# Differential attention on one core: v and z of a head pair projected together in row layout, rows gated before they are transposed, the weighting of values moved into the next pair

## The reference

```
proj = u @ w_in                                  # 2048 x 8192: q | k | v | z
logits = q_h @ k_h.T * scale + bias, causal      # 16 heads of 128 columns
p = softmax(logits)                              # two heads make a pair
a = p[:, :, 0] - lam * p[:, :, 1]
o = rms_norm(a @ v, subln_g) * (1 - lam_init)    # v: 256 columns for each pair
y = (o * silu(z)) @ w_out
h = layer_norm(alpha * x + y, ln_g, ln_b)
```

## Time and profile before

| | |
|---|---|
| median of 3 runs | 979.56 us (979.45 to 979.62) |
| profiled execution | 979.38 us |
| its span, first to last instruction | 977.6 us |
| TensorE busy | 963.7 us, 99% |
| VectorE busy | 449.1 us, 46% |
| ScalarE busy | 310.5 us, 32% |
| GpSimd busy | 66.4 us, 7% |
| granted TensorE clock, mean | 0.996 |

### The profile page before, as it was taken

How to read it: one execution, slowest core, us unless ns; L and a number is a source line. 1 busy time by engine, 2 the same in 40 slices (tenths; PEclk the granted TensorE clock), 3 DMA queues, 4 the chain that set the end, 5 groups by cost and what they waited for, 6 DMA issues and landing times.

```text
span 977.6 us, 13295 instructions
## 1 busy us (share of the span) xinstructions
PE 963.7 (99%) x5200; PEld 836.1 (86%) x5200; DVE 449.1 (46%) x694; ACT 310.5 (32%) x493; POOL 66.4 (7%) x137
## 2 busy tenths in 40 slices
PE   9999999999999999999999999999999999999995
PEld 7898889888988898889888988898889888888884
DVE  4634443454345434543454345334533475425465
ACT  4424322432243224322432243223322453122200
POOL 2000100010001000100010001000100010000044
PEclk9999999999999999999999999999999999999998
DMA  8722422242224222322242224222322224442432
GB/s 293 269 89 84 135 87 88 85 134 86 86 86 134 86 86 86 134 86 86 86 135 86 86 86 134 86 86 86 107 86 86 86 76 139 174 149 87 150 115 101
DMA packets 32790, 108.63 MB, mean 111 GB/s; under 512 B 4208, under 2 KB 5232, under 8 KB 32512
## 3 DMA queue, kind: packets, MB, share of 16 engines
q1 hardware_dynamic: 28320, 94.65, 28.3%
q0 software_dynamic: 2336, 9.48, 2.9%
q10 hardware_dynamic: 2112, 4.19, 1.3%
HBM read 104.07 MB, written 9.48 MB: 116 GB/s over the span
## 4 chain that ended last, share of the span: by engine, by line
PE 98%; ACT 0%; POOL 0%; DMA 0%; DVE 0%; issue 0%; POOLq 0%; ACTq 0%
PE proj L774 81%; PE att L774 15%; PE att L858 1%; PE att L883 1%; DMA big<-x_cols_dram 0%; POOL big L384 0%; POOLq L73 0%; POOL var_eps L376 0%; ACT x_res L418 0%; ACT w_split L525 0%; ACT scratch L416 0%; ACT big L539 0%; DVE stats L726 0%; DVE big L723 0%; DVE xg_split L555 0%
## 5 line engine op out<-in xcount | busy, mean ns | idle before, releaser
L774 PE MATMUL proj<-xg_split,w_split 128*128 128x512 f32 x2304 | 539.9, 392 | 0.4 <-DVE w_split L668 0.3
L774 PEld LDWEIGHTS proj<-xg_split,w_split 128*128 128x128 f32 x2304 | 428.4, 188 | 87.8 <-DVE xg_split L555 0.6
L549 DVE TENSOR_TENSOR w_split<-w_raw,w_split 128x1024 fp32r<-128x1024 f32 x128 | 156.8, 1225 | 279.9 <-ACT w_split L397 279.0
L397 ACT ACTIVATE w_split<-w_raw 128x1024 fp32r<-128x1024 f32 x128 | 135.6, 1059 | 442.6 <-PE proj L774 434.0
L774 PE MATMUL proj<-w_split,xg_split 128*128 128x256 f32 (+1 forms) x1872 | 265.3, 302 | 0.0
L774 PEld LDWEIGHTS proj<-w_split,xg_split 128*128 128x128 f32 x1872 | 249.4, 191 | 13.5
L591 DVE CUSTOM_DVE_ANT_0 scratch<-att,bias 128x128 f32<-128x128 f32 (+3 forms) x64 | 28.9, 489 | 108.4 <-PE att L774 108.4
L774 PE MATMUL att<-operands 128*128 128x256 f32 (+2 forms) x432 | 71.2, 303 | 0.0
L774 PE MATMUL att<-w_split,xg_split 128*128 128x512 f32 x288 | 66.1, 389 | 0.0
L774 PEld LDWEIGHTS att<-operands 128*128 128x128 f32 x432 | 61.5, 190 | 3.1
L774 PEld LDWEIGHTS att<-w_split,xg_split 128*128 128x128 f32 x288 | 54.1, 188 | 11.2
(11 more groups left out here) (73 smaller groups left out, 409.1 us busy)
## 6 DMA issues: line engine op xcount, KB each, us to landing
w_raw<-w_in_tiles_dram SPq DMA_DIRECT2D x126, 512.0 KB, 3.3
w_raw<-w_out_tiles_dram SPq DMA_DIRECT2D x32, 512.0 KB, 3.3
bias_by_distance<-bias_lines POOLq DMA_DIRECT2D x8, 640.0 KB, 6.4
bias<-bias_by_distance POOLq DMA_DIRECT2D x8, 512.0 KB, 5.4
x_res<-in_x_dram ACTq DMA_DIRECT2D x4, 1024.0 KB, 5.1
big<-x_cols_dram SPq DMA_DIRECT2D x7, 512.0 KB, 9.8
out_dram<-big SPq DMA_DIRECT2D x4, 512.0 KB, 2.7
out_dram<-big SPq DMA_DIRECT2D x8, 256.0 KB, 2.5
```

Of the source, the lines that this page charges most:

```text
L397: nc.scalar.activation(split_view(a, 0), w_raw[:, ring(a)], ACT.Copy).then_inc(w_hi, 1)
L549: nc.vector.tensor_tensor(split_view(a, 1), w_raw[:, ring(a)], split_view(a, 0).bitcast(F32), ALU.subtract).then_inc(w_ready, 1)
L774: return nc.tensor.matmul(dst, lhsT, rhs, start=start, stop=stop, skip_group_check=True)
```

## The change

1. v and z of a pair are made together. Their weight tiles are stored anew: 8 tiles of two blocks of 128 rows, each 512 columns wide, 256 of v and 256 of z. `vz_part` (quarters j = 8 to 15) keeps rows of x stationary and moves 512 columns, 24 matmuls a quarter, for one block of rows s after another; block s has the whole bank s of `proj`. So z is now in row layout too.
2. The gate is applied to rows: `gate` on DVE reads the weighted values from PSUM, the row norm's scale and silu(z), and writes `gated`; ACT's second pass over the weighted values is gone. Then `turn_gated` transposes two blocks at once, and ACT copies them to `g` with the gain `subln_g` (`g_copy`).
3. `weigh_v` of a pair moves to quarters 0 to 3 of the next pair, `turn_a` for t = 2, 3 to its quarters 0 and 1, `turn_gated` to 3 and 5. `turn_a` for t = 0, 1 stands after quarter 12.
4. ACT copies z, exp(-z) and v of a block as soon as the block is finished (`vz_tiles`), DVE the lo part of v. k is moved head by head.
5. `scores_of(0)` makes 128 columns.
6. In the layer norm `var_eps` goes from POOL to DVE, the gain is copied by ACT into the `proj` banks and for the last block the bias into `att`, and the DVE's pieces are 512 + 1024 columns (centre) and 3 x 512 (scale).
7. The last pair's slots are written out after the loop on DVE and ACT, with the first splits of g in slot 14.

The core of the diff:

```diff
-                    if c == 2:
-                        for s in range(ST):
-                            rows = slice(s * P, (s + 1) * P)
-                            dst = proj[:, bank + s // 2, (s % 2) * PW:(s % 2 + 1) * PW]
-                            mm(dst, x_hi[:, rows], w[0][:, kk], first and s % 2 == 0, False)
-                            mm(dst, x_hi[:, rows], w[1][:, kk], False, False)
-                            last = mm(dst, x_lo[:, rows], w[0][:, kk], False, final and s % 2 == 1)
+            def vz_part(p, j):
+                part = j - VZ
+                pe.wait_ge(w_ready, p * QUARTERS + j + 1)
+                w = [split_view(j, l).rearrange("p (k n) -> p k n", k=VK) for l in range(2)]
+                for s in range(ST):
+                    if part == 0:
+                        if s == 0:
+                            pe.wait_ge(q_moved, p + 1)
+                        elif s >= 2:
+                            pe.wait_ge(k_moved, 2 * p + s - 1)
+                    rows = slice(s * P, (s + 1) * P)
+                    dst = proj[:, s]
+                    for kk in range(VK):
+                        k = part * VK + kk
+                        x_hi, x_lo = xg_split[:, 0, k, rows], xg_split[:, 1, k, rows]
+                        mm(dst, x_hi, w[0][:, kk], k == 0, False)
+                        mm(dst, x_hi, w[1][:, kk], False, False)
+                        last = mm(dst, x_lo, w[0][:, kk], False, k == KT - 1)
...
+                if part == 0 and not opening:
+                    pe.wait_ge(vz_moved, p * ST - 2 + 2 * c)
...
-                n = max(t + 1, 2) * P
+                n = (t + 1) * P
...
             def late_inserts(p, j):
-                if j == 0:
-                    weigh_v(p, 3)
-                if j < 4:
-                    turn_normed(p, j)
+                if j < ST:
+                    weigh_v(p, j)
+                if j < 2:
+                    turn_a(p, j + 2)
+                if j in (3, 5):
+                    turn_gated(p, j // 2 - 1)
 
             def own_inserts(p, j):
                 if 9 <= j < 13:
                     scores_of(p, j - 9)
-                if 11 <= j < 15:
-                    turn_a(p, j - 11)
-                if 13 <= j:
-                    weigh_v(p, j - 13)
+                if j == 12:
+                    turn_a(p, 0)
+                    turn_a(p, 1)
...
+            def vz_tiles(p):
+                for s in range(ST):
+                    if s < ST - 1:
+                        act.wait_ge(vz_done, p * (ST - 1) + s + 1)
+                    else:
+                        act.wait_ge(quarter_done, (p + 1) * QUARTERS)
+                    nc.scalar.activation(silu_z[:, s], proj[:, s, PW:2 * PW], ACT.Exp, scale=-1.0)
+                    nc.scalar.activation(z_rows[:, s], proj[:, s, PW:2 * PW], ACT.Copy)
+                    nc.scalar.activation(v[:, 0, s], proj[:, s, 0:PW], ACT.Copy).then_inc(vz_hi, 1)
...
+                dve.wait_ge(o_scale_ready, n)
+                dve.wait_ge(silu_ready, n)
+                nc.vector.scalar_tensor_tensor(gated[:, t], av, o_scale[:, t:t + 1], silu_z[:, t],
+                                               ALU.mult, ALU.mult).then_inc(gated_ready, 1)
...
-                pool.wait_ge(mv_ready, s + 1)
-                nc.gpsimd.tensor_scalar(var_eps[:, s:s + 1], mean_var[:, s, 1:2], 1.0, EPS,
-                                        ALU.mult, ALU.add).then_inc(var_ready, 1)
...
+                nc.vector.tensor_scalar(var_eps[:, s:s + 1], mean_var[:, s, 1:2], EPS, None, ALU.add
+                                        ).then_inc(var_ready, 1)
...
                     nc.vector.scalar_tensor_tensor(r_rows[:, s, cols], r_rows[:, s, cols], mean_var[:, s, 0:1],
-                                                   ln_g_all[:, cols], ALU.subtract, ALU.mult).then_inc(centred, 1)
+                                                   bank_cols(g_banks, cols), ALU.subtract, ALU.mult
+                                                   ).then_inc(centred, 1)
```

More of the change, by code:

```diff
@@ L216, in chunk_part, with turned_a @@
         def chunk_part(p, j):
-            if isinstance(p, int) and p == 0 and j < 8:
+            if isinstance(p, int) and p == 0:
                 return j % 2, j // 2
-            return j // 4, j % 4
+            return j // QK, j % QK
+        def turned_a(t):
+            return turned[:, P:3 * P] if t == 1 else turned[:, 0:(t + 1) * P]
         def x_unit_of(k):
@@ L430, in aT_split @@
                     act.wait_ge(av_done, p * ST + t - 1)
-                act.wait_ge(aT_done, p * ST + t + 1)
-                nc.scalar.activation(aT[:, t % 2, 0, 0:(t + 1) * P], turned[:, 0:(t + 1) * P],
-                                     ACT.Copy).then_inc(aT_hi, 1)
+                act.wait_ge(aT_done, p * ST + max(t, 1) + 1)
+                nc.scalar.activation(aT[:, t % 2, 0, 0:(t + 1) * P], turned_a(t), ACT.Copy).then_inc(aT_hi, 1)
             def norm(p, t):
-                if t == 0 and not (isinstance(p, int) and p == 0):
-                    act.wait_ge(g_ready, p * ST)
@@ L446, in late_steps, with g_copy @@
-            def late_steps(p, j):
-                if j == 0:
[L449 to L453, removed]
+            def g_copy(p, i):
+                act.wait_ge(nT_done, 2 * p + i + 1)
+                for e in range(2):
+                    src = turned.rearrange("p (t e s) -> p e t s", t=2, e=2)[:, e]
+                    dst = g[:, bass.ds(p * 2 + e, 1), 2 * i * P:2 * (i + 1) * P]
+                    last = nc.scalar.activation(dst.rearrange("p k (t s) -> p (k t) s", t=2), src, ACT.Copy,
+                                                scale=sub_g[:, e:e + 1])
+                last.then_inc(g_ready, 1)
@@ L454, in own_steps, with slot @@
+            def late_steps(p, j):
+                if j in (1, 2):
+                    aT_split(p, j + 1)
+                if 1 <= j <= 4:
+                    norm(p, j - 1)
+                if j in (4, 6):
+                    g_copy(p, j // 2 - 2)
+            def slot(p, j, late):
+                if j == VZ:
+                    k_chunk(p)
+                split_hi_at(p, j)
+                if late:
+                    late_steps(p - 1, j)
                 if j == (7 if isinstance(p, int) and p == 0 else 4):
-                    chunk(p, 0)
@@ L456, in own_steps, with g_early_hi @@
-                if j in (8, 12):
-                    chunk(p, j // 4 - 1)
+                    q_chunk(p)
+                if j == 13:
+                    aT_split(p, 0)
+                    aT_split(p, 1)
                 if 10 <= j < 14:
                     exps(p, j - 10)
[L460 to L463, removed]
+            def g_early_hi():
+                act.wait_ge(g_ready, (PAIRS - 1) * 2)
+                act.wait_ge(scores_done, PAIRS * ST)
+                for i in range(EARLY // 2):
+                    nc.scalar.activation(g_early[:, 0, 2 * i:2 * i + 2], g[:, 2 * i:2 * i + 2],
+                                         ACT.Copy).then_inc(g_hi, 1)
@@ L535, in _ @@
                         load_res(act, c)
-            for s in range(ST):
+            act.wait_ge(ln_loaded, 32)
+            act.wait_ge(r_ready, (CHUNKS - 1) * ST)
+            for c in range(CHUNKS):
+                last = nc.scalar.activation(g_banks[:, c], ln_g_all[:, c * NC:(c + 1) * NC], ACT.Copy)
+            last.then_inc(ln_moved, 1)
+            for s in range(ST):
+                if s == ST - 1:
+                    act.wait_ge(r_ready, CHUNKS * ST - 1)
+                    for c in range(CHUNKS - 1):
+                        last = nc.scalar.activation(b_banks[:, c], ln_b_all[:, c * NC:(c + 1) * NC], ACT.Copy)
+                    last.then_inc(ln_moved, 1)
                 act.wait_ge(shift_ready, s + 1)
@@ new lines, in k_chunk, with vz_tiles @@
+            def k_chunk(p):
+                for e in range(2):
+                    dve.wait_ge(k_hi, 2 * p + e + 1)
+                    nc.vector.tensor_tensor(kT[:, 1, e], proj[:, 2 + e], kT[:, 0, e].bitcast(F32),
+                                            ALU.subtract).then_inc(k_moved, 1)
+            def vz_tiles(p):
+                for s in range(ST):
+                    dve.wait_ge(vz_hi, p * ST + s + 1)
+                    nc.vector.tensor_tensor(v[:, 1, s], proj[:, s, 0:PW], v[:, 0, s].bitcast(F32),
+                                            ALU.subtract).then_inc(vz_moved, 1)
@@ L600, in combine @@
                 n = p * ST + t + 1
-                if not (isinstance(p, int) and p == 0):
-                    dve.wait_ge(normed_ready, n - ST)
                 dve.wait_ge(exp_ready, n * 2)
@@ L964 @@
 G_ORDER = [*G_STEPS.values(), *G_REST]
-VECTOR_PIECES = [slice(0, D // 2), slice(D // 2, 3 * D // 4)]
+CENTRE_PIECES = [slice(0, NC), slice(NC, 3 * NC)]
+VECTOR_PIECES = [slice(c * NC, (c + 1) * NC) for c in range(CHUNKS - 1)]
 POOL_PIECE = slice(3 * D // 4, D)
```

269 lines of the change are left out of this document (139 added, 130 removed).

## The result

The changed kernel takes 968.52 us (median of 4, 968.31 to 968.76) against 979.55 for the kernel before (979.45 to 979.62): a ratio of 0.9888, interval 0.987 to 0.9905, 11.0 us less. 967.5 was predicted. The profiled execution took 968.76 us, its span is 966.8.

What follows compares the result with a forecast made beforehand. TensorE was taken to bound the eight pairs, and a chain over DVE, POOL, ACT and DMA the end. Terms -10.0 - 0.5 + 0 + 0.8 - 2.3 = -12.0 us gave 967.5 us, range 964.7 to 974.6 (forecast's own 964.7 to 969.5).

Steps and rivals of the forecast that it cites:

- Part 1: v and z quarters of each pair: 96 matmuls fewer save 1.25 us a pair, 10.0 us in all (9.4 to 11.3).
- Part 2: Scores of t = 0: 48 matmuls go from 256 to 128 columns at the transposes' 110 ns, -0.5 us.
- both other prices: For a 128-column matmul: 66 ns by a straight line through 256 and 512 columns, or plain float32's 236 (472 a matmul).
- Part 3: Steps moved within the loop: their results come before TensorE wants them, thinnest cover 0.6 us at the first gate; 0 us.
- T + 2.5: T is the start of the next pair's quarter 0; ACT's last block and the weight split end 2.5 us later.
- Part 4: Last pair's seam with the output product: a 1.4 us wait for the gate replaces one of 0.6; +0.8 us (0.0 to 1.6).
- Part 5: Kernel's end, layer norm: power starts earlier and POOL's two steps take 1.12 us each; -2.3 us (-1.1 to -2.6).
- cheap end: The forecast with the cheap ends of parts 1, 2 and 5: 964.8 us.
- the narrow form: Rivals on the 128-column scores: 236 ns a matmul gives 973.6 us, chance 0.35; 472 ns gives 984.9, chance 0.04.
- the loop's gate: Rival: DVE's queue to the first gate is late in every pair, +13 us, 980.8 at most; chance 0.05.
- columns alone: Rival: columns alone set the matmul time, so the joined v and z quarters gain about 0, 977.5 us; chance 0.03.

Runs made afterwards that it cites:

- cut matmuls: The changed kernel with each joined matmul of 512 columns cut into two of 256, same order of work: 987.29 us.
- in bulk: The changed kernel with quarter 10 of every pair cut into pieces of 128 columns, 96 matmuls instead of 24: 1010.22 us in one run.

## Why the prediction was right

**Part 1, v and z together.** Predicted 1.25 us a pair, 10.0 in all. A pair came out 1.27 to 1.28 us shorter (8.92 / 7), the joined quarters at 5.45. The cut matmuls show the step itself: 12.2 ns a matmul, where 12 to 13 were read from the earlier trace rows. The Trainium skill's 2.5 ns ("TensorE: Matmul & The Clock Gate", section "Back-to-back issue gap") is given there for isolated matmuls and does not hold for this stream; 1536 matmuls at that price would have cost 3.8 us, and they cost 18.8.

**Part 2, the narrow scores.** Predicted -0.5 by the transposes' 110 ns; in bulk it is 112. The choice of the nearest row was right, and both other prices are excluded; but nearness was the only reason given, so that the two agree so well is in part luck. What the term lacked is that the next group gives nearly all of it back (5.54 for 5.47): the gain is nil within what the runs can tell.

**Part 3, the cover.** The queue to the first gate was worked out to end 0.6 us ahead of its need, more with overlap. The timeline of DVE in the changed kernel, the first split of the queue and the gate:

```profile
197.76 1.23 DVE L591 TENSOR_TENSOR w_split<-w_raw,w_split 128x1024 fp32r<-128x1024 f32 x1 [0.52 <-ACT w_split L414]
...
205.59 0.48 DVE L670 SCALAR_TENSOR_TENSOR scratch<-att,o_scale,scratch 128x256 f32<-128x256 f32 x1
```

The gate ends at 205.59 + 0.48 = 206.07, 1.19 us ahead of the six matmuls that want it, which start at 207.26 (1.36 ahead of the end of the quarter before, 207.43). The steps of silu, split and scale took what their rows said. Quarter 0 starts at 195.65, so the queue began 0.4 us sooner than the T + 2.5 of the working, and its steps overlap by 0.2. The banks for quarters 0 and 8 were never waited for. The added reciprocal shows that there was little room here, 1.1 us; that every other place has more was not tried.

**Part 4, the seam.** Predicted a wait of 1.4 us for one of 0.6, +0.8; measured 1.07 of idle and 0.24 of lost overlap, 1.25 by the pair of runs with and without it, for 0.6: +0.7. The cause is the one named, since it goes when the gates stand ahead of the splits. (Of the two splits of g in that queue, the first, from 778.16, runs just ahead of the first row of the order listing of the changed kernel; that listing shows only the second.)

**Part 5, the end.** This term was mis-sized: -2.3 predicted, -1.7 measured, -1.6 by the end alone. POOL was set free as worked out, but its steps take 1.27 us and not 1.12, twice 0.15; and the last transfer takes 966.8 - 963.33 - 0.45 = 3.0 us behind its issue where it was 2.6. The run with the end alone shows 3.0 too, so this comes with the new end; why it lands later was not tried. The working's 2.65 is 0.03 above its own terms (1.22 + 0.93 + 0.47). The Trainium skill's rule on the shared port ("SBUF — State Buffer", section "SBUF: two separate sides") agrees with the runs: with one operand in PSUM DVE takes 2.06 us beside POOL's work, with both in SBUF 4.08. By it 2.65 would have been won; 1.7 were.

The rest of the difference, some 0.5 us, lies in the start: the two v quarters that pair 0 works off before its first scores should have given 0.6, and 0.12 came out, because TensorE's second piece of work began at 12.91 us instead of 12.39, with the first loads of x. The runs here differ by such amounts: the first scores of pair 0 begin between 61.42 and 62.15 us in five traces whose work up to there is that of the changed kernel, and at 62.27 and 62.65 in the two with that of the kernel before. The profiled run of the changed kernel is the latest of the five, so this is not taken for an effect of the change.

One slip in the sum changed nothing: its cheap end was added up with 10.3 us for part 1, whose own range ends at 11.3, so the range should have begun 1.0 us lower than at 964.7.

None of the rivals came: the narrow form is not slow, the loop's gate is in time, and columns alone do not set the time.

## What to carry to other kernels

When TensorE's chain fills the time, count matmuls as well as columns: in this stream each pays about 12 ns beside its columns down to 256, and below that the price hardly falls (112 ns at 128 columns). Joining two products that can share the stationary operand, so that one matmul of 512 columns stands for two of 256, takes matmuls away (288 to 192 a pair for v and z here), if the engines that empty the banks keep up; work out the queue of the one engine on which the moved steps meet, slot by slot, and put the step that TensorE waits for ahead of splits that are wanted quarters later. And where POOL and VectorE work side by side on the critical end, put one operand of VectorE's steps into PSUM.

## What the runs showed of the hardware

A wait costs more than its length: 0.41 us of idle cost 0.65 us a pair. Without a wait the next six matmuls start 0.17 us before the quarter ahead of them has ended and take 0.87 us; behind it they take 0.95.

In the profiled run with the extra reciprocal TensorE stood still for 2.67 us at the seam, and the next quarter behind it took 7.05 instead of 5.47 us. The stretches before, behind and after it (us, busy times, clock in the third column from the end):

```profile
788.00:794.70 6.70, 4.08 (x18) 3.01 (x17) 6.60 (x10) 1.90 (x2) 0.74 (x2) 1.00 0.03 7
794.70:798.00 3.30, 3.25 (x15) 2.87 (x16) 3.23 (x4) 1.76 (x4) 0.62 (x1) 0.70 0.43 150
798.00:803.20 5.20, 5.20 (x22) 4.21 (x21) 5.10 (x9) 0.23 (x1) 1.65 (x2) 0.86 0.30 101
```

The granted clock fell to 0.70 and 0.86 in the means of the two stretches, so for a part of them to 1.2 of 2.4 GHz, after it had been 1.00. After the 1.07 us wait of the changed kernel it stayed at 1.00. That execution took 976.08 us at a mean granted clock of 0.994, the three others of this kernel 973.92 to 974.52 at 0.997 to 0.998. The difference is about the 1.58 us that the slowed quarter lost, so the clock most likely did not fall in those; they left no trace to show it.
